# A two-layer decoder trunk on one core: the second token half's stages placed between the first half's expert units

## What is computed

```
for l in range(DEPTH):                       # DEPTH = 2
    if l % 2 == 0:  x = x + even_mixer(...)  # GLA and stick-breaking attention
    else:           x = x + odd_mixer(...)   # causal attention and a gated linear recurrence
    x = x + memory_cross_attention(...)      # 4 heads into 256 memory tokens
    x = x + peer_ffn(...)
def peer_ffn(xn, wq, subkeys, u, v):
    ...
    s = jnp.einsum('thcd,hcnd->thcn', q, subkeys)
    s1, i1 = lax.top_k(s[:, :, 0], K)        # K = 16
    s2, i2 = lax.top_k(s[:, :, 1], K)
    cand = (s1[..., :, None] + s2[..., None, :]).reshape(Tb, PEER_HEADS, K * K)
    top_s, pos = lax.top_k(cand, K)
    ...
    act = jax.nn.gelu(jnp.einsum('td,thkd->thk', xi, u[eidx]), approximate=False)
    return jnp.einsum('thk,thkd->td', g * act, v[eidx])
```

## Time and profile before

| | |
|---|---|
| median of 3 runs | 1933.07 us (1929.7 to 1933.99) |
| the profiled execution's own time | 1930.56 us |
| its span, first to last instruction | 1928.8 us |
| granted TensorE clock, mean of the span | 0.984 of full speed |
| busy: PE, DVE, ACT, POOL | 1591.4, 1011.3, 646.9, 514.9 us |
| DMA | 610.20 MB, mean 316 GB/s over the span |

### The profile page before, as it was taken

One profiled execution on the slowest core, in us unless ns is written; L12 is line 12 of the kernel. 1 busy time (PEld: TensorE's weight loads), 2 busy tenths in 40 slices (PEclk: granted clock), 3 DMA queues, 4 the chain that ended last, 5 costly groups with the idle time before them and its releaser, 6 DMA issues.

```text
span 1928.8 us, 15560 instructions
## 1 busy us (share of the span) xinstructions
PE 1591.4 (83%) x4638; PEld 806.3 (42%) x4638; DVE 1011.3 (52%) x2487; ACT 646.9 (34%) x1897; POOL 514.9 (27%) x516
## 2 busy tenths in 40 slices
PE   7999989767877877787779989997788777877876
PEld 4777778222322222222237666763232222222222
DVE  3432238688544554445441632489874445444454
ACT  1243221423433333333332433123343333333333
POOL 0000001434433433333300000015444343333331
PEclk9999999999999999999989999999999999999999
DMA  8321224999999999999933222359999999999996
GB/s 304 131 88 44 101 108 184 390 416 421 422 421 422 421 422 422 421 421 422 421 154 131 88 104 93 118 221 422 421 421 421 422 421 421 422 421 422 421 421 287
DMA packets 107540, 610.20 MB, mean 316 GB/s; under 512 B 10032, under 2 KB 10176, under 8 KB 41280
## 3 DMA queue, kind: packets, MB, share of 16 engines
q0 software_dynamic: 73728, 536.90, 67.1%
q1 hardware_dynamic: 33728, 72.30, 10.3%
HBM read 608.12 MB, written 1.05 MB: 316 GB/s over the span
## 4 chain that ended last, share of the span: by engine, by line
DMA 45%; PE 38%; DVE 9%; ACT 5%; issue 2%; POOL 0%; SPq 0%; DVEq 0%; PEldq 0%; ACTq 0%
DMA arena<-in_experts,idxT 45%; PE psum L516 37%; DVE arena L1416 5%; ACT cst L882 1%; ACT gains L882 1%; ACT arena L882 1%; ACT gelus L882 1%; ACT L882 1%; DVE red L1385 1%; DVE kv L1377 0%; POOL arena L1710 0%; DMA vecs<-in_vecs 0%; ACT sqb L882 0%; DVE kv L1383 0%; DVE red L1200 0%
## 5 line engine op out<-in xcount | busy, mean ns | idle before, releaser
L516 PE MATMUL psum<-arena,cst 128*128 128x512 f32 (+2 forms) x2112 | 1029.4, 616 | 283.6 <-ACT cst L882 279.1
L1416 DVE CUSTOM_DVE_ANT_0 arena<-arena,xrow 128x1024 f32<-128x1024 f32 x512 | 624.4, 1224 | 537.7 <-DMA arena<-in_experts,idxT 537.0
L1710 POOL DMA_INDIRECT arena<-in_experts,idxT x512 | 514.7, 1005 | 1387.8 <-PE psum L516 790.0
L516 PEld LDWEIGHTS psum<-arena,cst 128*128 128x128 f32 x2112 | 367.1, 191 | 942.5 <-ACT cst L882 645.7
L882 ACT ACTIVATE gelus<-red 128x1 f32<-128x1 f32 x512 | 103.6, 202 | 770.2 <-DVE red L1416 769.9
L516 PE MATMUL psum<-hT,ring 128*128 128x256 f32 x1280 | 293.3, 390 | 6.1 <-DVE hT L1215 6.1
L516 PEld LDWEIGHTS psum<-hT,ring 128*128 128x128 f32 x1280 | 248.9, 196 | 47.5 <-issue 9.8
L882 ACT ACTIVATE cst<-cst,gains 128x128 f32<-128x128 f32 x512 | 206.2, 403 | 23.2 <-PE psum L516 6.7
L882 ACT ACTIVATE gains<-gelus,gateT 128x1 f32<-128x1 f32 x512 | 150.8, 294 | 17.0 <-ACT gelus L882 0.2
L882 ACT ACTIVATE arena<-psum 128x512 f32<-128x512 f32 (+3 forms) x89 | 47.8, 545 | 304.3 <-PE psum L516 304.0
L516 PE MATMUL psum<-mixT,ring 128*128 128x256 f32 x256 | 57.4, 387 | 2.5 <-DVE mixT L1689 2.5
(11 more groups left out here) (161 smaller groups left out, 672.1 us busy)
## 6 DMA issues: line engine op xcount, KB each, us to landing
ring<-in_peer_wq SPq DMA_DIRECT2D x8, 2048.0 KB, 8.1
ring<-in_ev_w_in SPq DMA_DIRECT2D x6, 2048.0 KB, 11.8
ring<-in_od_w_in SPq DMA_DIRECT2D x5, 2048.0 KB, 33.0
ring<-in_xa_wkv SPq DMA_DIRECT2D x4, 2048.0 KB, 7.9
arena<-in_experts,idxT POOLq DMA_INDIRECT x512, 15.3
ring<-in_ev_w_out SPq DMA_DIRECT2D x2, 2048.0 KB, 7.8
ring<-in_xa_wq SPq DMA_DIRECT2D x2, 2048.0 KB, 9.2
ring<-in_xa_wo SPq DMA_DIRECT2D x2, 2048.0 KB, 7.7
```

The lines of the kernel that those rows point to most:

```text
L516: return nc.tensor.matmul(out, lhsT, rhs, start=start, stop=stop)
L1416: V.tensor_tensor_reduce(out=ut, in0=ut, in1=xrow[:, u // PAIRS, :], scale=1.0, scalar=0.0, op0=ALU.mult, op1=ALU.add, accum_out=dots[:, k ...
L1710: nc.gpsimd.indirect_dma_start(slot[slot_of(u)], None, d["experts"], bass.IndirectOffsetOnAxis(ap=idxT[:, u:u + 1], axis=0))\
```

## The change

Tokens are treated in two halves, t = 0 and t = 1, from layer 0's cross-attention on (the even mixer stays as it is). There are four gathers of 128 units, q = 0 to 3 (layer 0 half 0, layer 0 half 1, layer 1 half 0, layer 1 half 1), as one stream of 512 units. All other work after the even mixer is cut into jobs on 128 token columns, and each job gets a *mark*, a unit number at which it is done: `units_to(mark)` does all units before it first. PE stands two units earlier than ACT and DVE (`PE_LAG`).

- While half 0's units of layer 0 run (units 0 to 127), cross-attention (marks 18 to 42) and routing (marks 44 to 84) of half 1 and layer 1's memory keys and values (88 to 104) are done.
- While gather 1 runs, half 0 goes through the odd mixer (marks 132 to 188), cross-attention (188 to 210) and routing (212 to 252) of layer 1; while gather 2 runs, half 1 does the same, 128 units later. Gather 3 has nothing beside it.
- In the stretches named by `on_vector`, every second unit's v part is scaled and added on DVE in `yacc` (`expert_sum`) and has no diagonal on ACT and no matmul on PE: 104 of the 512 units. `sum_up` adds the PSUM sum and `yacc`.
- For layer 1 PE starts the sum with `xT` transposed by the identity, so that `yacc` is the output in token order, and the last half is written out in two pieces.
- Weights from the cross-attention on are loaded once for each half. The ring has four slots of 1 MB; the host lays each block out so that a partition's part is one run of 8 KB (before: runs of 2 KB). There are 71 blocks of 1 MB after the first list of experts is ready, counted from the list.
- 6 rotating PSUM banks in place of 8, two banks fixed for the sum, 7 slots in place of 8; ACT loads a function set whenever the next function needs another (`table`).

```diff
-BANKS = 8
+BANKS = 6
...
-BLOCK = 4096
+BLOCK = 2048
...
-SLOTS = 8
-UNITS = PAIRS * TT
+GATHERS = LAYERS * TT
+UNITS = GATHERS * PAIRS
+SLOTS = 7
 DIAGS = 4
+ACC_BANK = BANKS
+PE_LAG, SUM_LAG = 2, 3
...
+    def peer(l, t):
+        for g in range(4):
+            for i in range(2):
+                add(f"pq{l}{t}.{g}_{i}", d[f"peer_wq{l}"][2 * g + i], f"pq{l}{t}.{g}")
+            add(f"sub{l}{t}.{g}", d["subkeys"][l][:, 4 * g * PE_KEYS:4 * (g + 1) * PE_KEYS], f"ps{l}{t}.{g}")
...
+def spread(marks, jobs, first, last):
+    total = sum(JOB_WEIGHT.get(j[:2], 2) for j in jobs)
+    done = 0
+    for j in jobs:
+        marks[j] = first + (last - first) * done // total
+        done += JOB_WEIGHT.get(j[:2], 2)
+def route_marks(q, g):
+    if q == 0:
+        return ([0, 0, 0, 0, 0], [0, 0, 0, 0, 0], [0, 2, 4, 6, 8], [8, 10, 12, 14, 16])[g]
+    m = (0, 44, PAIRS + 84, 2 * PAIRS + 84)[q] + 10 * g
+    return [m, m + 3, m + 6, m + 7, m + 10]
+def unit_marks(jobs):
+    marks = {name: 0 for name in jobs}
+    spread(marks, cross_jobs(0, 1), 18, 42)
+    for q in range(1, GATHERS):
+        for name in peer_jobs(q // TT, q % TT):
+            marks[name] = route_marks(q, int(name[-1]) if "." in name else 0)[0]
+    spread(marks, KEY_JOBS, 88, 104)
+    for t in range(TT):
+        at = (t + 1) * PAIRS
+        spread(marks, [f"back{t}.0", f"back{t}.1"] + odd_jobs(t), at + 4, at + 60)
+        spread(marks, cross_jobs(1, t), at + 60, at + 82)
+    return marks
+def on_vector(u):
+    q, k = divmod(u, PAIRS)
+    if q == 0:
+        return k % 2 == 1 and (18 <= k < 42 or 84 <= k < 104)
+    return q < 3 and k % 2 == 1 and k < 82
...
+            def expert_unit(u):
+                if ON_V[u]:
+                    return
+                q, i = u // PAIRS, PE_COUNT[u]
+                begins, ends = i == PE_COUNT[q * PAIRS], PE_COUNT[u + 1] == PE_COUNT[(q + 1) * PAIRS]
+                if begins:
+                    if q:
+                        pe.wait_ge(summed_up, q)
+                    if q >= TT:
+                        t = q - TT
+                        copied(pe, f"xo1{t}.0", f"xo1{t}.1")
+                        for c in range(KC):
+                            mm(acc[:, c // 4, c % 4 * P:(c % 4 + 1) * P], xT[:, c, tok(t)], ident, c % 4 == 0, False)
+                pe.wait_ge(weighed, i + 1)
+                v = slot[slot_of(u)][:, D:2 * D]
+                first = begins and q < TT
+                mm(acc[:, 0, :], diag[:, i % DIAGS, :], v[:, 0:BANK], first, ends)
+                mm(acc[:, 1, :], diag[:, i % DIAGS, :], v[:, BANK:D], first, ends).then_inc(expert_mm, 1)
+            def units_to(n):
+                while next_unit[0] < n:
+                    expert_unit(next_unit[0])
+                    next_unit[0] += 1
...
+                units_to(UNIT_AT[name] - PE_LAG)
...
+            def quarters(name, rhs, norm=None):
+                o, done = job(name)
+                for j in range(4):
+                    w = weights(f"{name}_{j // 2}")
+                    for k in range(KC):
+                        if norm and j == 0:
+                            pe.wait_ge(h_ready, KC * TILE_NORM[norm] + k + 1)
+                        last = mm(o[:, j * P:(j + 1) * P], w[:, k, j % 2 * P:(j % 2 + 1) * P], rhs[:, k, :],
+                                  k == 0, k == KC - 1)
+                last.then_inc(done, 1)
...
+            def table(which):
+                if loaded[0] != which:
+                    load_table(which)
+                    loaded[0] = which
...
+                def exponentials(g):
+                    units_to(route_marks(q, g)[3])
+                    act.wait_ge(top_ready, 4 * q + g + 1)
+                    table(LN_EXP)
+                    fn(top[:, 2 * g:2 * g + 2, :], top[:, 2 * g:2 * g + 2, :], ACT.Exp).then_inc(top_exp, 1)
...
+            def expert_dot(u):
+                q, k = divmod(u, PAIRS)
+                landed(dve, u)
+                ut = slot[slot_of(u)][:, 0:D]
+                V.tensor_tensor_reduce(out=ut, in0=ut, in1=xrow[:, q % TT, :], scale=1.0, scalar=0.0,
+                                       op0=ALU.mult, op1=ALU.add, accum_out=dots[:, k:k + 1]).then_inc(dotted, 1)
...
+            def expert_sum(u):
+                q, k = divmod(u, PAIRS)
+                y, v, g = yacc[:, q % TT, :], slot[slot_of(u)][:, D:2 * D], gains[:, k:k + 1]
+                dve.wait_ge(gain_done, u + 1)
+                if V_COUNT[u] == V_COUNT[q * PAIRS]:
+                    ins = V.tensor_scalar(y, v, g, None, ALU.mult)
+                else:
+                    dve.wait_ge(expert_add, V_COUNT[u])
+                    ins = V.scalar_tensor_tensor(y, v, g, y, ALU.mult, ALU.add)
+                ins.then_inc(expert_add, 1)
...
+            def sum_up(q):
+                y = yacc[:, q % TT, :].rearrange("p (b n) -> p b n", n=BANK)
+                gather_taken(dve, q)
+                added = V_COUNT[(q + 1) * PAIRS]
+                if added > V_COUNT[q * PAIRS]:
+                    dve.wait_ge(expert_add, added)
+                    V.tensor_tensor(y, y, acc, ALU.add).then_inc(summed_up, 1)
...
+            def units_to(n):
+                while next_unit[0] < n:
+                    u = next_unit[0]
+                    expert_dot(u)
+                    if u >= SUM_LAG and ON_V[u - SUM_LAG]:
+                        expert_sum(u - SUM_LAG)
+                    if u >= PAIRS and u % PAIRS == SUM_LAG - 1:
+                        sum_up(u // PAIRS - 1)
+                    next_unit[0] += 1
...
+                    mark = route_marks(q, g)
+                    best_keys(g)
...
+                    units_to(mark[1])
                     candidates(2 * g, 2)
                     best_pairs(2 * g, 2)
...
+                    units_to(mark[2])
                     ranks(2 * g, 2)
...
+                    units_to(mark[3])
+                    chosen(2 * g, 2)
+                    units_to(mark[4])
                     if g:
...
+            for u in range(UNITS):
+                q, k = divmod(u, PAIRS)
+                if k % 32 == 0:
+                    pool.wait_ge(idx_ready, 4 * q + k // 32 + 1)
+                if u >= SLOTS:
+                    taken(pool, u - SLOTS)
```

1768 lines of the change are left out of this document (877 added, 891 removed).

## The result

The change makes the kernel slower: 1988.44 us in the median (1985.44 to 1993.03, 4 runs) against 1931.39 of before beside it, a ratio of 1.0298 with a 95% interval of 1.0283 to 1.0314. The forecast was 1815 us, in a range of 1765 to 1890.

A forecast was written before the change was run, and what follows sets the result against it. DMA was taken to bound the two gathers, PE and chains the rest; after the change, DMA nearly throughout. Floor 1751.6 us plus 60 of stops gave 1811.6; with the run's time above its span, 1815 us, range 1765 to 1890.

The forecast's parts named there:

- the floor: Whole kernel without stops: first list 283.7, start 8 and 1.5, DMA stream 1449.4, end 9, together 1751.6 us.
- The routing chain: Woven routings: PE, ACT, DVE chain of 35.6 us a group against DMA's 30.4; 26 us a window, 78 for three.
- So: 78 less reserves of 12.4, 8 and 8 gives 50: Three routing windows: 78 us of chain loss, cut to 50 by lists that DMA still has in hand.
- The five lists in hand: Gather stream when DVE stands: DMA still has some five lists with 7 slots, about 12.4 us of work.
- Together 170 us: even with DMA: Odd mixer: DVE's work and waits add up to 170 us against DMA's 174; only 5 us charged for each mixer.
- the cross-attention gives a little back: Woven cross-attention: 65 us of DMA against 60 of DVE, so no loss there.
- The certain price: Weights in the stream cost 177 us, more than half loaded a second time; certain as long as DMA is the limit.
- the handover itself: Rival "slower": each of 129 jobs stops PE, ACT and DVE, reserve takes none; 2014 us at 2 us each; chance 0.05.
- Chains bind everywhere: Rival: mixer waits twice as long, crosses behind too; 37 us more per mixer, 15 per cross, 1885 to 1930; chance 0.11.
- The sets: Rival: ACT's 79 more function set loads hold the stream; 1916 us with all in the path, 1866 with half; chance 0.02.
- Weights late: Rival: weight blocks land late in the odd mixers; 40 to 55 us on top, 1855 to 1870; chance 0.12.
- three dips: Sign: GB/s row at 410 or more from about 290 us to the end, except in three routing windows.

The follow-up runs named there:

- Run 5: Run 2's kernel with marks of their own for each engine in the three woven routings: 1854.5 us, ratio to before 0.9607.
- Run 2: The changed kernel with the sum of a DVE unit one dot behind its own dot in place of three: 1934.4 us, ratio to before 1.0018.
- run 11: Run 5's kernel with six slots in place of seven: 1920.1 us, ratio to before 0.9946.
- run 15: Run 2's kernel with a load of another function set ahead of each set load at a change on ACT: 2007.1 us, ratio to before 1.0390.
- Run 6: Run 2's kernel with an eighth of the columns in the projections' second weight load, 83 us of transfer left out: 1918.8 us, ratio to before 0.9943.
- Run 14: Run 5's kernel with own marks in mixer and cross too, and the mixer's ten attention jobs further apart: 1830.2 us, ratio to before 0.9481.
- run 8: Run 2's kernel with a PE product with zeros ahead of units in the first three quarters: 1951.9 us, ratio to before 1.0120.

## Why the prediction was wrong

**What was right: the floor's parts.** The first list is ready at 285.0 us (POOL's wait for it; forecast 283.7). The last gather runs at 422 GB/s. The sum of 1024 columns takes 1283 ns (forecast 1.3 us). From the last dot to the end there are 8.2 us (forecast 9):

```profile
L1294 DVE SCALAR_TENSOR_TENSOR yacc<-arena,gains,yacc 128x1024 f32<-128x1024 f32 x101 | 129.6, 1283 | 1.5 <-ACT gains L972 1.4
```

```profile
1979.21 1.23 DVE L1283 CUSTOM_DVE_ANT_0 arena<-arena,xrow 128x1024 f32<-128x1024 f32 x1 [1.22 <-DMA arena<-in_experts,idxT]
```

The first dot begins at 306.5 us, 21.5 behind the list; but the dots stand behind DVE's own routing work, and the DMA engines began sooner:

```profile
285.00:290.00 5.00, 4.27 (x38) 4.05 (x37) 4.90 (x32) 0.60 (x1) 3.63 (x4) 1.00 0.82 295
290.00:295.00 5.00, 2.82 (x26) 2.63 (x24) 3.42 (x28) 0.00 (x0) 3.09 (x4) 1.00 1.01 420
295.00:300.00 5.00, 3.92 (x23) 3.92 (x24) 4.21 (x14) 0.23 (x1) 0.00 (x0) 0.73 0.99 357
300.00:306.50 6.50, 2.68 (x19) 2.33 (x17) 6.29 (x37) 1.88 (x2) 0.00 (x0) 0.94 1.01 425
```

What they moved by the first dot is 19.2 us of work at 422 GB/s, so they lost 2.3 us at the start. The floor had 8 us of idle DMA and 1.5 us to the first byte, two terms that no row showed; POOL's first issue is at 285.45 us and the first packet of a gather at 287.2. By the packets the DMA engines then lose 235 us between the first and the last dot, of which the table by dots shows 226.4. (Of the readings of before, one is off without a consequence: the earlier trace rows has 11 and 12 slices at 421 to 422, not 13 each.)

**The routing chain was right, in place and size.** A group after the first takes 34.9 to 36.9 us, 35.9 in the mean, forecast 35.6, and DVE stands 10 us for the scores in each. Only the first group is longer, 48 us for 41: DVE stands 7.4 us for the norm there, and the queries take 9.1, 10.1 and 9.1 us at a granted clock of 0.81, 0.72 and 0.81, where those at 1.00 take 7.3. 103 us in three windows, against the 78 that I had before the reserves. Run 5 shows that the loss goes when DVE and PE's scores come later.

**The step that failed: "So: 78 less reserves of 12.4, 8 and 8 gives 50".** None of the 28 us shows in the time. The five lists in hand were read off a landing of 16.2 us, over 2.485. But that row is of 300 to 440 us, where 8 MB of weights flowed among the gathers. From 450 to 900 us, by the packets, a list of the kernel before takes 11.7 us from issue to landing (median), and 4.6 are on the way in the mean, with eight slots. At the routing stops of the changed kernel it is three, and one landed; in the timeline above the DMA engines work on for 7.2 us. At the first stop of a window and in the mixers and crosses one reason is that a unit summed on DVE keeps its slot for three more dots, and POOL issues in order. At the other nine routing stops no such unit is near, and the slots are held by units that wait for PE. And a reserve can help only once in a window: with 35.9 us of chain against 30.4 of transfer in each group it is used up, and to fill it again there is no time: between two stops, from 470 to 488 us, the DMA engines are already at 421 to 429 GB/s. Run 2 puts the late sum at 54 us and run 11 one slot at 66. In the sum this step is 53 of the 176 us that were missed.

**"Together 170 us: even with DMA" and "the cross-attention gives a little back" failed too, and together cost more: 72 and 32 us.** An engine's busy time and its waits added up to less than DMA's time, and I took that for cover. The terms themselves were right. In the first mixer DVE is busy for 127.9 us and waits 36.6 for PE and ACT, forecast 133 and 37. What the sum lacks are DVE's waits for gathers behind its stops:

```profile
DVE arena L1283 <- DMA arena<-in_experts,idxT: 41.8, 17, 5.0
DVE xT L1351 <- PE psum L581: 12.4, 2, 8.1
```

(The waits of DVE from 727.4 to 939.4 us, the two largest.) In the cross-attention behind it these waits are 15.0 us in 83. So the mixer's work on DVE and the transfers don't run side by side throughout: when DVE goes on, the gathers that its stop held up have not landed, and it waits once more. The mixers took 38 and 44 us over DMA, forecast 5 each, the crosses 5.8, 13.4 and 12.9, forecast below nothing. With several stops of 9 to 12 us and three lists in hand, what counts isn't the sum over a stage but each stop against the reserve. Of these 114 us the early sum took 42, thinner weights 16 more in one mixer; attention further apart took 14 of what was left; the sets are on its chain (run 15). I had charged 5 us for them in each mixer.

**The certain price was not one.** All weights behind the first list were 177 us of my floor, more than half of it the second load. Run 6 leaves out 83 us of transfer and gives 16 back.

**The rivals.** By its range, the last came true, the handover itself, at a chance of 0.05: it decided from 1.4 us per job, and 235.8 us over the floor are 1.8 us for each of the 129 jobs. Against it I had put the reserve of 12.4 us and PE's two units in hand. By its mechanism it holds in part. It had every stop lost whole; but at each routing stop 3 to 4 gathers are still moved, and one slot is worth 66 us (run 11). And 54 us are of the late sum, which no rival named and which a handover doesn't bring: they go with the same jobs at the same marks (run 2). *Chains bind everywhere* (0.11) had the places: it put 37 us more on each mixer and 15 on each cross, and measured are 33 and 39 more, and 6 to 13 over DMA for a cross. Its reason, waits twice as long, isn't borne out: in the first mixer they are 36.6 us as forecast. Its top of 1934 us kept the reserves in the routings; with the 53 us of these it would stand at 1987. That is close in part by chance, since the crosses lose less than it said and other stages more. The sets had 0.02; added loads cost 0.72 us each. Weights late: no, PE waited 3.3 us for the ring, all told. Instead of three dips the GB/s row is low from 350 to 1640 us.

**What stays open.** Run 14 still takes some 80 us more than the floor, 37 of them in the first 36 units of the two mixers and 20 in the routings, where its DMA engines are full (421 GB/s), so that transfers put off earlier may be made up there. And what PE's clock alone costs: I had not thought of it at all, and run 8 only shows that raising it with more work doesn't pay. A part can be read: the 26 projections of 32 matmuls from 430 us on take 7.3 us each at a clock of 1.00 and 12 us more than that in all. An early clock would save up to that there, if nothing else binds; what the slower products of units cost isn't shown.

## What to carry to other kernels

Before you weave two streams, count what is in flight at the moment an engine stops: slots less those that are held between landing and release, in the order in which the issuing queue takes them. What a stop is longer than that is lost, however idle the engines are in the mean. A second stop that comes before the reserve is filled again finds less of it. At a mark where work changes engines, don't let the consumer arrive at the same unit as the producer: with marks of their own for PE, ACT and DVE, an early release and linked jobs further apart, the same change went, in run 14, from 3.0% slower to 5.2% faster than the kernel before.
